# Last block's output projection: seven of eight tiles in 512-column matmuls of the high weights

## What is computed

```python
def moba_mixer(h, w_in, w_out, rel_table):
    q, k, v = jnp.split(h @ w_in, 3, axis=-1)
    ...
    return (o @ w_out).astype(h.dtype)

def swiglu(h, w13, w2):
    g, u = jnp.split(h @ w13, 2, axis=-1)
    return ((jax.nn.silu(g) * u) @ w2).astype(h.dtype)
...
        h = h + y                                                       # y: the mixer's output
        h = h + swiglu(rms_norm_2(h, norm_ffn[layer]), ffn_w13[layer], ffn_w2[layer])
    return rms_norm_2(h, final_norm)
```

## Time and profile before

| | us |
|---|---|
| time, median of 3 (1142.43 to 1142.56) | 1142.52 |
| time of the profiled execution | 1142.97 |
| its span, first to last instruction | 1141.1 |
| PE busy | 1130.6 |
| DVE busy | 870.1 |
| ACT busy | 665.0 |
| POOL busy | 383.0 |

### The profile page before, as it was taken

The page is one execution under the profiler, slowest core; times in us unless marked ns, Lnnn a source line. Parts: engine busy times, 40 slices in busy tenths (PEclk is TensorE's granted clock), DMA queues, the critical chain, the costliest instruction groups (busy, mean ns, idle before and its releaser), DMA issues.

```text
span 1141.1 us, 23482 instructions
## 1 busy us (share of the span) xinstructions
PE 1130.6 (99%) x8304; PEld 1039.8 (91%) x8304; DVE 870.1 (76%) x1364; ACT 665.0 (58%) x1127; POOL 383.0 (34%) x387
## 2 busy tenths in 40 slices
PE   9999999999999999999999999999999999999997
PEld 9999999989999999899979988888888898888886
DVE  6968897987699888448877787777666877777753
ACT  6687657655576666446557665555555555555453
POOL 3468000602246664222000344445220025444431
PEclk9999999999999999999999999999999999999999
DMA  7676434676355556653645365557655445556662
GB/s 263 192 216 209 134 116 131 202 240 209 128 184 185 184 184 182 202 188 103 194 148 168 111 188 186 190 188 261 205 188 182 147 135 180 186 187 190 204 204 78
DMA packets 56851, 204.55 MB, mean 179 GB/s; under 512 B 6881, under 2 KB 7305, under 8 KB 56657
## 3 DMA queue, kind: packets, MB, share of 16 engines
q1 hardware_dynamic: 54576, 196.96, 54.6%
q0 software_dynamic: 1920, 6.28, 1.9%
q10 hardware_dynamic: 288, 0.39, 0.1%
HBM read 200.95 MB, written 2.63 MB: 178 GB/s over the span
## 4 chain that ended last, share of the span: by engine, by line
PE 95%; DVE 3%; ACT 1%; issue 1%; DVEq 0%; ACTq 0%
PE bank L1643 26%; PE bank L1644 15%; PE bank L1649 13%; PE bank L1650 13%; PE bank L1651 13%; PE bank L1646 3%; PE bank L1777 2%; PE bank L1779 2%; PE bank L1778 2%; PE bank L1697 1%; DVE w_lo L856 1%; PE bank L1880 1%; PE bank L1870 1%; PE bank L1747 1%; PE bank L1902 1%
## 5 line engine op out<-in xcount | busy, mean ns | idle before, releaser
L856 DVE TENSOR_TENSOR w_lo<-raw,w_hi 128x1024 fp32r<-128x1024 f32 x370 | 465.8, 1262 | 113.4 <-ACT w_hi L351 108.5
L351 ACT ACTIVATE w_hi<-raw 128x1024 fp32r<-128x1024 f32 x370 | 389.4, 1054 | 137.7 <-PE bank L1644 59.8
L1649 PE MATMUL bank<-h_two,w_hi 128*128 128x256 f32 x1072 | 310.2, 289 | 0.7 <-ACT work L487 0.3
L1650 PE MATMUL bank<-h_two,w_hi 128*128 128x256 f32 x1072 | 303.2, 283 | 0.0
L1651 PE MATMUL bank<-h_two,w_lo 128*128 128x256 f32 x1072 | 303.2, 283 | 0.0
L1643 PE MATMUL bank<-h_two,w_hi 128*128 128x512 f32 x714 | 257.8, 400 | 0.2 <-DVE h_two L887 0.2
L1644 PE MATMUL bank<-h_two,w_lo 128*128 128x256 f32 x816 | 212.7, 281 | 0.0
L1649 PEld LDWEIGHTS bank<-h_two,w_hi 128*128 128x128 f32 x1072 | 205.4, 192 | 4.6 <-issue 2.9
L1650 PEld LDWEIGHTS bank<-h_two,w_hi 128*128 128x128 f32 x1072 | 205.5, 192 | 0.6
L1651 PEld LDWEIGHTS bank<-h_two,w_lo 128*128 128x128 f32 x1072 | 205.4, 192 | 0.0
L1643 PE MATMUL bank<-u_two,w_hi 128*128 128x512 f32 x574 | 203.5, 397 | 0.0
(11 more groups left out here) (256 smaller groups left out, 1601.5 us busy)
## 6 DMA issues: line engine op xcount, KB each, us to landing
raw<-in_stream SPq DMA_DIRECT2D x372, 512.0 KB, 3.6
u_two<-u_two POOLq DMA_DIRECT2D x4, 384.0 KB, 5.7
bias_rows<-bias_row POOLq DMA_DIRECT2D x1, 1536.0 KB, 15.1
work<-in_x_t SPq DMA_DIRECT2D x2, 512.0 KB, 5.4
work<-in_x_t POOLq DMA_DIRECT2D x1, 1024.0 KB, 6.3
work<-bias_rows POOLq DMA_DIRECT2D x1, 1024.0 KB, 9.7
work<-bias_rows POOLq DMA_DIRECT2D x1, 512.0 KB, 5.7
out<-work SPq DMA_DIRECT2D x2, 256.0 KB, 2.5
```

What stands on the lines that cost most here:

```text
L351: A(w_hi[:, slot, :], raw[:, slot, :], ACT.Copy).then_inc(hi_ready, 1)
L856: v.tensor_tensor(w_lo[:, slot, :], raw[:, slot, :], w_hi[:, slot, :].bitcast(F32), ALU.subtract).then_inc(lo_ready, 1)
L1649: mm(out, w_hi[:, slot, s], r_two[:, 0, :], start=start, stop=False)
L1650: mm(out, w_hi[:, slot, s], r_two[:, 1, :], start=False, stop=False)
```

## The change

The tiles 0 to 6 of `mo` are written wide, tile 7 stays narrow. ACT and DVE get the low half to copy and to add, as in the other wide stages: the conditions in `feed` and `add_branch` that let only stages of three parts a tile do so are widened, and the count of low halves (`LOW_BEFORE`) gets seven more entries. Inside `tile` and `three` nothing is changed.

```diff
--- before.py
+++ after.py
@@ -301,7 +301,7 @@
             SCANS.setdefault(H_FOX + 5 + 3 * t // 2, []).append(t)
         LOW_BEFORE, _n = {}, 0
         for name, n_tiles in (("pb", C), ("pa", C - 1), ("down", C - 1), ("up1", 2 * F2), ("down1", C - 1),
-                              ("mqk", 2 * C - 2), ("up2", 2 * F2), ("down2", C - 1)):
+                              ("mqk", 2 * C - 2), ("mo", C - 1), ("up2", 2 * F2), ("down2", C - 1)):
             LOW_BEFORE[name] = _n
             _n += n_tiles
         HALVES = {"up1": 0, "up2": 2 * F2}
@@ -752,8 +752,8 @@
 
                 for j in range(per * C):
                     multiplied(PART[name] + j)
-                    if per == 3 and j % 3 == 2 and j // 3 < C - 1:
-                        low_half(TILE[name] + j // 3)
+                    if name != "ho" and j % per == per - 1 and j // per < C - 1:
+                        low_half(TILE[name] + j // per)
                     if j < per * C - 1:
                         hi(0, 0, PART[name] + j + HI_AHEAD)
                     if j % per == per - 1:
@@ -1384,7 +1384,7 @@
                     if j % per == 0 and t >= 1 and norm != "final":
                         h_low(norm, t - 1)
                     if j % per == per - 1:
-                        if per == 3 and t < C - 1:
+                        if t < C - 1:
                             dve.wait_ge(low_out, LOW_BEFORE[name] + t + 1)
                             low = LOW[:, (TILE[name] + t) % BANKS, :]
                             chain.wait(v.tensor_tensor(X[:, t, :], X[:, t, :], low, ALU.add))
@@ -2089,7 +2089,7 @@
             moba_values(6)
 
             def first(t, blocks):
-                tile(0, PART["mo"] + t, TILE["mo"] + t, u_two, y_lo, C, blocks)
+                tile(0, PART["mo"] + t, TILE["mo"] + t, u_two, y_lo, C, blocks, wide=True)
 
             first(0, range(0, 6))
             first(1, range(0, 3))
@@ -2102,7 +2102,7 @@
             for t in range(3):
                 first(t, range(7 if t < 2 else 4, BLK))
             for t in range(3, C):
-                tile(0, PART["mo"] + t, TILE["mo"] + t, u_two)
+                tile(0, PART["mo"] + t, TILE["mo"] + t, u_two, wide=t < C - 1)
             after_norm("f1", "up2", 2 * F2, wide=True)
             down("down2", F2, F1 + F2)
             stat("final")
```

## The result

The change makes the kernel slower: 1146.08 us as the median of 8 runs (1145.33 to 1147.17), beside 1142.55 for the kernel before in the same session (8 runs, 1142.38 to 1142.89). The ratio is 1.0031, with an interval of 1.0022 to 1.0040; the difference is 3.5 us. The forecast was 1145.2 in a range of 1142.5 to 1146.5. The profiled execution of the kernel after took 1146.59 us with a span of 1144.7, against 1142.97 and 1141.1 before. Its whole stretch around `mo` begins 0.24 us earlier than in the trace of before, so 0.24 is to be added where one of its times is held against one of before.

What follows compares the result with a forecast made beforehand. PE was taken to bound the kernel (95% of the chain), with DVE deciding in mo. A 2.62 us shift of up2's block 7 plus 0.10 for a waited matmul gave +2.7 on 1142.52: 1145.2, range 1142.5 to 1146.5.

Steps and rivals of the forecast that it cites:

- PE's saving: In mo, 56 wide blocks each save the seam of one matmul: 0.36 to 0.67 us, taken as 0.36.
- DVE's series: In mo, seven added low-half adds, held by POOL, lengthen DVE's cycle a tile from 2.44 to 3.21 us.
- T0, T1, T2 and T7: Forecast starts of DVE's bank add L1393 for mo's tiles 0, 1, 2 and 7; the last at 951.92, before 947.09.
- whoever stands waiting goes next: POOL and DVE exclude each other on operations with two SBUF inputs; a held L1390 takes 0.96 us.
- What PE sees: At up2, PE waits for w_lo from 945.7 to 948.1, then for h_low(7); block 7 shifts by 2.62 us.
- main case: DVE's held adds in mo make PE wait in up2: +2.7 us, 1145.2, chance 0.62.
- rival B: PE's clock falls to 1.2 GHz in the wait from 945.7: +3.7 to +7.3, taken as 1147.7, chance 0.08.
- a w_lo of 1.42 us: Slow end in mo: w_lo keeps its present length, DVE's cycle is 3.41 us, the time 1146.2.
- Rival A: In mo, DVE's adds get in ahead of POOL: cycle 2.78 us, +0.6, time 1143.1, chance 0.21.
- Rival C: DVE's additions in mo hide and the gain stays: 1141.9 to 1142.2 us, chance 0.09.
- Queues at no cost: Around mo and up2, SP's later loads cost nothing; bank reuse after tile 5's add (946.9) comes ahead of 948.1.

Runs made afterwards that it cites:

- e2_no_squares: The changed kernel without POOL's squares of tiles 0 to 6 of mo, so the norm reads only part of its input: 1142.03 us, ratio 0.9995.
- e3: The kernel before, mo all narrow, plus one more DVE operation with two SBUF inputs in each of tiles 0 to 6: 1145.23 us, ratio 1.0025.
- e1_fill: The changed kernel with matmuls of ones, read by nobody, on PE where it stands still ahead of up2: 1145.43 us, ratio 1.0026.
- e8_lead: The changed kernel with PE doing five blocks of up2's first tile before waiting for the second part's w_lo: 1145.42 us, ratio 1.0025.
- e6_last4: The changed kernel with only tiles 3 to 6 of mo wide, tiles 0 to 2 and 7 narrow: 1143.94 us, ratio 1.0012.
- e7_swap: The changed kernel with each wide mo tile's two adds swapped, bank first, low half second: 1143.46 us, ratio 1.0010.
- after_again: The changed kernel unaltered, run once more in another session on another chip: 1146.27 us, ratio 1.0032.

## Why the prediction came out as it did

- **PE's saving:** right. 0.353 us a wide block against 0.360 is 0.4 us for 56; I took 0.36. PE is through with `mo` at 945.35 (the start of its last matmul and the 0.12 that one costs), 945.59 with the earlier start, against 945.70. In e2_no_squares, where DVE is not late, the saving comes out as 0.40.
- **DVE's series:** right, and it is the heart of it. Forecast T0, T1, T2 and T7 were 930.82, 933.65, 936.86 and 951.92; with 0.24 added, the trace has 930.78, 933.62, 936.84 and 951.95. The held L1390 (0.96), the w_lo of 1.22 where it was 1.42, and the cycle (3.21 forecast, 3.23 measured) are those worked out by the rule that whoever stands waiting goes next. e2 and e3 show from both sides that DVE's operation and POOL together are the cause, ACT's copies and the wide matmuls are not.
- **What PE sees:** the profile gives 2.56 us for the wait for w_lo, from the end of the last matmul at 945.51. Counted as I did, from 945.35, it is 2.72, where I had 2.4: PE comes to it 0.11 us earlier, and starts 0.25 us behind w_lo's end and not 0.06. With the clock kept (e1_fill, e8_lead) the loss is 2.8 us in the median, where the main case had 2.7. The wait for h_low of tile 7 is 0.22 to 0.25 in the profiles of e1_fill and e3_adds_only, and 0.4 counted as I did, where I had 0.5; the later start of `up2` takes up the rest.
- **The step that fell short:** the sum of the main case left the clock at its full level, and I gave rival B only 0.08. It happened together with the main case, in both traces of the change and, by the mean clock, in 8 of its 14 executions. The earlier trace rows had shown a fall behind a wait of about this length, and I set it aside because nothing there told how the clock would behave when PE goes on. Of B's price the low end was right: I had +3.7 for four slow blocks less 0.5 hidden in the wait for h_low, and the runs show +3.5 and +3.7. The term was mis-sized in its parts: four blocks took 0.64 us each and not 0.72, and the ones beside them 0.48 and 0.61. The value that I took for B, 1147.7, was too high.
- **The range:** that 1146.08 lies inside it is in part luck. The upper end of 1146.5 was there for a w_lo of 1.42 us, which did not happen; most of the 0.9 us over the 1145.2 of the main case came from the clock. And I wrote that the range leaves out B, although B's low end, 1142.52 + 3.7 = 1146.2, lies in it.
- **Rival A** fell: all of L1390 from tile 2 on is held. e7_swap comes out near its numbers, with a cycle of 2.77 us against 2.78 and a loss of 0.9 us in the median (0.5 in the trace) against 0.6. But it gets there by another order of events: there the bank's add goes first and w_lo isn't held. **Rival C** fell, as PE's saving is there but lies in front of the wait.
- **Queues at no cost:** right for SP; PE shows no wait for a part's DMA in the stretch. The bank of tile 5's add didn't bind in the change, but is what binds next when the wait for w_lo is moved (e8_lead), and I hadn't ranked it.

What stays open: why the medians of e6_last4 and e7_swap are 0.3 and 0.4 us above what their traces show, and why the clock falls in some executions of one and the same kernel and not in others.

## What to carry to other kernels

When a change moves work from the engine that bounds the kernel to one that follows it, count that engine's cycle a tile with the new instruction in it, and with the operations of a third engine that share its memory ports: the slack at the end of the stage (here 2.1 us), and not the share of busy time, decides. An operation that reads SBUF twice is best put where the other engine is idle; swapping it with its neighbour that reads PSUM cut the loss here from 3.7 to 0.9 us (medians of one session). And a new wait on TensorE can cost more than the lateness that causes it: behind the wait of 2.5 us here, a fallen clock added another 0.9 to 1.1 us in more than half of the executions. Before times of two traces are compared, see where both start the stretch: here the starts lie up to 1.05 us apart.

## What the runs showed of the hardware

- **The clock.** After PE had stood still for 2.56 us (2.54 in after_again), the granted clock was 0.50, the 1.2 GHz level, from 950 to 952 us (0.69 and 0.60 in the windows beside); it had first stayed at 1.00 for a good microsecond of matmuls. In after_again it was 0.56 already in 948 to 949 us: it is still 1.00 from 948.0 to 948.1 and 0.50 from 948.2 on, so it had fallen before PE's first matmul at 948.61. It was 0.73 in 951 to 952 and 1.00 after. In the profiled executions it stayed at 1.00 after a wait of 1.98 us in e3_adds_only and after 1.27 us with two of 0.59 in e8_lead. But by the means of whole executions (0.996 or 0.997 against 0.998 or more) it fell somewhere in three of the ten of e3_adds_only and in one of the eleven of e7_swap, and in none of the eleven of e8_lead.
- **A slow block has no seam.** At the low level a block takes 0.64 us, which is just 768 columns at 1.2 GHz. The Trainium skill (TensorE: Matmul & The Clock Gate, "Wait — 56ns, not 53.3ns?") gives a distance of N / 1.2 ns for the slow clock and N / 2.4 + 2.5 for the fast one; the traces agree with the first, and show 353 ns where the second gives 325.
- **DVE and POOL take turns by whole instructions.** POOL's L1565 of 256 columns takes 0.61 us alone and 1.46 behind a w_lo, and ends 0.47 us after it; a DVE add of 0.42 takes 0.95 behind POOL's sum, and ends 0.28 us after it. That the one which already stands waiting goes next is what the forecast of the cycle was worked out by, 3.21 us, and the trace has 3.23.
